# One-core hybrid block: order of the difference tables around the coefficient store, place of one output weight slice, order of two ScalarE copies at the start

## The reference, cut to what matters

```
h      = rmsnorm(x) * (1 + scale) + shift          # scale, shift, gate from silu(c) @ w_ada
u_pool, z_pool, u_ssm, z_ssm, g_pool, g_ssm = split(h @ w_in)
y_pool = pool_mixer(u_pool) * silu(z_pool)
y_ssm  = s5_mixer(u_ssm) * silu(z_ssm)             # complex diagonal state space, gelu, GLU
merged = sigmoid(g_pool) * (y_pool @ w_branch_pool) + sigmoid(g_ssm) * (y_ssm @ w_branch_ssm)
out    = x + gate * rmsnorm(merged @ w_out)
```

## Time and profile before

| | us |
|---|---|
| median of 3 runs | 964.11 |
| lowest and highest | 963.69, 964.80 |
| the profiled execution: its time | 963.69 |
| the profiled execution: its span | 961.9 |
| TensorE busy in the span | 940.3 |
| VectorE, ScalarE busy | 652.8, 349.9 |

### The profile page before, as it was taken

The page is one execution under the profiler, slowest core; times in us unless marked ns, Lnnn a source line. Parts: engine busy times, 40 slices in busy tenths (PEclk is TensorE's granted clock), DMA queues, the critical chain, the costliest instruction groups (busy, mean ns, idle before and its releaser), DMA issues.

```text
span 961.9 us, 11612 instructions
## 1 busy us (share of the span) xinstructions
PE 940.3 (98%) x4448; PEld 789.5 (82%) x4448; DVE 652.8 (68%) x914; ACT 349.9 (36%) x406; POOL 45.6 (5%) x82
## 2 busy tenths in 40 slices
PE   3999999999999999999999999999999999999997
PEld 3888878888888888888888888888888888788886
DVE  5988889988888868876797767654344444455233
ACT  6741442233333334545454554622022221133111
POOL 0019700000000000000000000000000000000000
PEclk9999999999999999999999999999999999999999
DMA  9753263445555379657566445895643264322222
GB/s 351 293 164 134 114 209 132 154 154 185 196 192 186 100 224 280 188 167 232 158 199 202 144 145 162 265 343 193 183 167 110 88 228 188 131 88 88 88 88 88
DMA packets 95687, 168.27 MB, mean 175 GB/s; under 512 B 37648, under 2 KB 54160, under 8 KB 95632
## 3 DMA queue, kind: packets, MB, share of 16 engines
q1 hardware_dynamic: 86272, 163.07, 50.8%
q10 hardware_dynamic: 9360, 4.46, 2.2%
HBM read 118.21 MB, written 49.28 MB: 174 GB/s over the span
## 4 chain that ended last, share of the span: by engine, by line
PE 97%; DVE 1%; DMA 1%; ACT 0%; issue 0%; SPq 0%; DVEq 0%
PE ps L1872 55%; PE ps L1979 17%; PE ps L2080 9%; PE psb L1979 5%; PE ps L2026 2%; PE psb L2015 1%; PE psb L2013 1%; PE psa L2001 1%; PE psa L1948 1%; PE psa L1872 1%; PE psb L1898 1%; DMA x_tok<-in_x 1%; PE psb L1948 0%; PE ps L1898 0%; PE psa L1898 0%; PE psa L2073 0%
## 5 line engine op out<-in xcount | busy, mean ns | idle before, releaser
L1872 PE MATMUL ps<-bop,w_hi 128*128 128x512 f32 x1312 | 352.3, 390 | 0.2 <-DVE bop L1372 0.2
L1872 PEld LDWEIGHTS ps<-bop,w_hi 128*128 128x128 f32 x1312 | 245.5, 188 | 51.0 <-issue 0.8
L1872 PE MATMUL ps<-bop,w_lo 128*128 128x512 f32 x656 | 202.0, 389 | 0.0
L1872 PEld LDWEIGHTS ps<-bop,w_lo 128*128 128x128 f32 x656 | 123.2, 188 | 25.7
L1324 DVE TENSOR_TENSOR w_lo<-raw,w_hi 128x1024 fp32r<-128x1024 f32 x49 | 60.4, 1232 | 59.9 <-ACT w_hi L989 59.7
L989 ACT ACTIVATE w_hi<-raw 128x1024 fp32r<-128x1024 f32 x49 | 51.7, 1057 | 92.4 <-PE ps L1872 82.6
L1979 PE MATMUL ps<-bop,r_hi 128*128 128x512 f32 x208 | 64.1, 389 | 0.0
L1979 PE MATMUL ps<-t_hi,r_hi 128*128 128x512 f32 x140 | 55.3, 395 | 0.3 <-issue 0.3
L1979 PE MATMUL ps<-t_hi,r_lo 128*128 128x512 f32 x140 | 54.6, 390 | 0.0
L1979 PE MATMUL ps<-t_lo,r_hi 128*128 128x512 f32 x140 | 54.5, 389 | 0.0
L2080 PE MATMUL ps<-wo_hi,y_hi 128*128 128x512 f32 x128 | 49.8, 389 | 0.0
(11 more groups left out here) (317 smaller groups left out, 1544.5 us busy)
## 6 DMA issues: line engine op xcount, KB each, us to landing
raw<-in_wstream SPq DMA_DIRECT2D x58, 512.0 KB, 5.4
pair_raw<-in_wstream SPq DMA_DIRECT2D x20, 512.0 KB, 4.6
ada<-in_w_ada SPq DMA_DIRECT2D x16, 512.0 KB, 11.4
x_tok<-in_x SPq DMA_DIRECT2D x8, 512.0 KB, 6.2
gs_d<-gt SPq DMA_DIRECT2D x8, 512.0 KB, 4.5
win_d<-win_new SPq DMA_DIRECT2D x8, 512.0 KB, 4.0
wout_d<-wout_new SPq DMA_DIRECT2D x8, 512.0 KB, 5.6
wout<-wout_d SPq DMA_DIRECT2D x8, 512.0 KB, 3.9
```

What stands on the lines that cost most here:

```text
L1872: last = mm(ps[slot(u)][:, f * HALF:f * HALF + HALF], a[:, k, :], b(k, f), start=k == 0 and q == 0, stop=k == KT - 1 and q == 2)
```

## The change

Four things change. `xt_out(6)` and `split_hi(2)` swap places on ScalarE. On ScalarE `t_high(2)` moves behind the first two `pair_high`. On VectorE `t_low(1)` and `t_sums(3)` move from ahead of the first two `pair_low` to behind them, `t_low(2)` moves ahead of `sum1`, and `t_low(3)` ahead of `sum4`. The hi part of slice 3 of `w_out` moves from the first weight buffer into `bop`, so that `wo_high(3)` and `wo_low(3)` come after the last `bs` product; the wait for `raw_free[0]` goes, and `squares` takes the first weight buffer.

```diff
--- before.py
+++ after.py
@@ -184,7 +184,7 @@
         w_hi = [new(f"w_hi{s}", [P, KT, P], F32R) for s in range(2)]
         w_lo_at = cur[0]
         w_lo = [new(f"w_lo{s}", [P, KT, P], F32R) for s in range(2)]
-        squares = at("squares", [P, SEQ], raw_at + 3 * TILE)
+        squares = at("squares", [P, SEQ], raw_at)
         gt_at = cur[0]
         gt = [new(f"gt{s}", [P, SEQ]) for s in range(2)]
         mod_out = at("mod_out", [P, 2, D], gt_at)
@@ -235,8 +235,8 @@
         wo_lo = at("wo_lo", [P, KT, D], b_at, F32R)
         wo_hi_big = at("wo_hi", [P, KT, D], bop_at, F32R)
 
-        wo_hi_first = [at(f"wo_hi{n}", [P, D], raw_at + o * TILE, F32R) for n, o in enumerate((2, 4, 1, 0))]
-        wo_hi = [t[:, :] for t in wo_hi_first] + [wo_hi_big[:, n, :] for n in range(4, KT)]
+        wo_hi_first = [at(f"wo_hi{n}", [P, D], raw_at + o * TILE, F32R) for n, o in enumerate((2, 4, 1))]
+        wo_hi = [t[:, :] for t in wo_hi_first] + [wo_hi_big[:, n, :] for n in range(3, KT)]
 
 
         p1 = [0]
@@ -1042,10 +1042,10 @@
             for k in range(2, KT):
                 h_of(k)
                 h_high(k)
+                if k == 2:
+                    split_hi(2)
                 if k in (2, 3):
                     xt_out(k + 4)
-                if k == 2:
-                    split_hi(2)
             act.wait_ge(h_done, KT)
             fn(eye_c[:, :, 0:P], ident.unsqueeze(1).broadcast_to((P, GB, P)), ACT.Copy).then_inc(eye_ready, 1)
 
@@ -1126,9 +1126,9 @@
                 fn(ks[:, 0:6, :].rearrange("p (a g) h -> p a g h", a=2), six[:, :, :, P:P + SG], ACT.Copy)
                 fn(ks[:, 6:GB, :], two_[:, :, P:P + SG], ACT.Copy).then_inc(k_taken, 1)
 
-            t_high(2)
             pair_high(0, P1)
             pair_high(0, P2)
+            t_high(2)
             t_high(3)
             act.wait_ge(gs_stored[0], 16 * 4)
             evac(("zs", 0), gt[0][:, :], ACT.Silu)
@@ -1286,10 +1286,10 @@
                     act.wait_ge(row_done, 1)
                     fn(gate_row[:, :], psa[:, :], ACT.Copy).then_inc(row_ready, 1)
             act.wait_ge(raw_free[1], len(USES) // 2)
-            act.wait_ge(raw_free[0], (len(USES) + 1) // 2)
-            for n in range(4):
+            for n in range(3):
                 wo_high(n)
             act.wait_ge(mm_done, JOB["bs", 7] + 1)
+            wo_high(3)
             wo_high(4)
             m_high(KT - 1)
             for n in range(5, KT):
@@ -1427,9 +1427,6 @@
             t_sums(1)
             t_low(0)
             t_sums(2)
-            t_low(1)
-            dve.wait_ge(tabled, 1)
-            t_sums(3)
 
             def bcast(ap, axis, n):
                 shape = list(ap.shape)
@@ -1588,12 +1585,15 @@
 
             pair_low(0, P1)
             pair_low(0, P2)
+            t_low(1)
+            dve.wait_ge(tabled, 1)
+            t_sums(3)
+            t_low(2)
             dve.wait_ge(coef_stored, 16)
             sum1(0)
             sum2(0)
+            t_low(3)
             sum4(0)
-            t_low(2)
-            t_low(3)
             for i in (P6, P5, P3, P4):
                 pair_low(0, i)
             sum3(0)
@@ -1805,7 +1805,7 @@
             def merge(n):
                 q, last = n % 2, n == KT - 1
                 if last:
-                    for t in range(4):
+                    for t in range(3):
                         wo_low(t)
                 dve.wait_ge(g_in[q], 16 * (n // 2) + 16)
                 dve.wait_ge(mm_done, JOB["bs", n] + 1)
@@ -1814,7 +1814,8 @@
                 dve.wait_ge(reload_in[q], 16 * (n // 2) + 16)
                 tt(rt[q][:, :], gt[q][:, :], rt[q][:, :], ALU.add).then_inc(m_sum, 1)
                 if last:
-                    wo_low(4)
+                    for t in range(3, 5):
+                        wo_low(t)
                 dve.wait_ge(m_hi_done, n + 1)
                 tt(m_lo[:, n, :], rt[q][:, :], m_hi[:, n, :].bitcast(F32), ALU.subtract).then_inc(m_lo_done, 1)
```

## The result

The changed kernel takes 970.75 us in the median of 6 runs (968.16 to 971.60), the kernel before beside it 964.77 (963.69 to 965.23). The ratio of the means over all runs, of which the changed kernel has eight, is 1.0057, 95% interval 1.0043 to 1.0070: slower by 0.6%, 6.0 us by the medians and 5.5 by the means, where 967.5 us were forecast (range 966.1 to 969.4). Slower was right; the size was too small and the time lies outside the range. The profiled execution took 970.14 us with a span of 968.4, against 963.69 and 961.9.

A forecast was written before the change was run, and what follows sets the result against it. TensorE, busy 940.3 of 961.9 us, was taken as the bound. 963.69 + 2.9 (first pair) + 0 (start) + 0.75 (end) = 967.3, or 967.8 from the median 964.11; predicted 967.5, range 966.1 to 969.4.

The forecast's parts named there:

- VectorE's stall: First pair: VectorE stands still from 120.8 to about 125.35, 4.6 us, because pair_low(0, P1) needs pair_high(0, P1).
- each step behind it: First pair: durations added on VectorE and ScalarE; table load to 134.6, P2 at about 135.7, P6 at 138.5.
- both paths meet at P6: First pair: VectorE's and ScalarE's paths both let P6 start at 138.5, so they are not added.
- The size without the clock: First pair: P6 starts 2.9 us later, bounds 2.0 to 3.8, with no fall of the clock counted.
- The end: Output tile 0: wo_low(3) behind the merge makes the weight load of k=5 late; +0.75 us, bounds 0.5 to 0.95.
- the edit of the first pair could win at most 0.68: First pair, before: matmuls miss the pace by 0.10 + 0.30 + 0.28 = 0.68 us, all an edit there could win.
- the rival of the clock: TensorE may restart at half rate after the first pair's gap: 1.8 us more, 969.3 us; chance 0.13.
- The forecast gap: TensorE waits 2.8 to 3.3 us ahead of P2 of the first pair, with none to speak of ahead of P6.
- this half microsecond is not added: Start: block 7's transposes come 0.5 us late, but the wait ahead of P2 shrinks from 3.3 to 2.8 us; counted 0.

The follow-up runs named there:

- e4: The changed kernel with the evacuation of zs 0 ahead of t_high(3) on ScalarE: 969.26 us, ratio 1.0054.
- e3: The changed kernel with 14 unread matmuls between P1 and P2 of the first pair: 968.83 us, ratio 1.0052.
- e8: The kernel before with t_low(2) and t_low(3) moved ahead of sum4 on VectorE: 963.67 us, ratio 0.9994.
- e6: The kernel before with only the new order of t_high, t_low and t_sums: 969.42 us, ratio 1.0053.
- e2: The changed kernel with the start's order of xt_out(6) and split_hi(2) put back: 968.88 us, ratio 1.0052.
- e1: The changed kernel again, no edit: 970.39 us, ratio 1.0069 against the kernel before.
- e10: The changed kernel without the start's swap, 13 unread matmuls ahead of P2, and 9 more on TensorE ahead of the third product: 969.55 us.
- e9: The changed kernel without the start's swap and with 13 unread matmuls in the gap ahead of P2: 968.56 us.
- e5: The kernel before with only xt_out(6) and split_hi(2) swapped: 964.85 us, ratio 1.0007.
- e7: The kernel before with only slice 3 of w_out moved: 964.85 us, ratio 1.0009.

## Why the prediction was right and wrong

**Right.** VectorE's stall (4.6 us forecast, 4.51 measured), its cause, and each step behind it: with 1.05 us added for the later start, the forecast has pair_high(0, P1) at 125.78 and it was at 125.75, the table load at 134.35 (134.47), P2 at 136.75 (136.93). That both paths meet at P6, to within 0.3 us, is shown by e4. The size without the clock is e3's: P6 103.25 us behind the transposes of block 7, before 100.27; 2.98, with 0.1 of it the longer transposes of block 7, and 2.9 were forecast. The end was forecast at 0.75 and is 0.76 in the trace. That the edit of the first pair could win at most 0.68 was right too (0.58 won in e8).

**Wrong: the rival of the clock.** "The clock falls" had a chance of 0.13; it happened, and it is the largest part of the error. Its price was put at 1.8 us and is 1.6 in e3 and 2.4 in e6. The range ended at 969.4, 0.1 above the clock's case alone, so it had no room for this case and anything beside it. The argument against it was that the gap is a fifth of the first idle time. That says nothing of how little idleness is enough. The forecast gap of 2.8 to 3.3 us was short by a little as well; it was 3.44. In the five profiles with a gap of microseconds the clock stayed up behind 2.86 (e4) and 3.04 us (e2) and fell behind 3.15 (e1) and twice behind 3.44 (the changed kernel, e6). Length alone doesn't decide, though: behind one length, 3.44 us, the clock was low from 137.6 in one kernel and from 134.66 in the other, and two runs of the changed kernel, 968.16 and 968.45 us, have a mean clock of 0.999, as the kernel before has. By the Trainium skill, page "TensorE: Matmul & The Clock Gate", "Part 1: The HAM clock gate", the array is at half clock after idleness. The traces agree where the clock fell, 0.59 behind the gap and 1.00 where it is filled; behind the gaps of e2 and e4 the profiled executions show no fall.

**Wrong: "this half microsecond is not added".** The step took the coefficient store as a fixed point, "whose start is set by coef's store and not by TensorE". The store hangs on GpSimd, GpSimd on VectorE's angles, and VectorE has split_lo(3) among them, which waits for ScalarE's split_hi(3), and that for TensorE's second product. The chain after shows this path, and e10 that it passes the 2.04 us on, to within 0.3. Before, this wait was just met and left no idle time to read. The other traces agree. From the transposes of block 6 to VectorE's split of tile 3 it is 30.83 to 30.89 us in the six kernels with the swap, with 0.41 to 0.57 us of idle time ahead of it, and 30.35 to 30.52 in the seven without it, with none; in e10, where TensorE is held back, VectorE stands idle there for 2.08 us. From block 6 to the store's issue it is 85.08 to 85.44 us with the swap and 84.55 to 84.97 without, 0.35 apart in the mean. So most of the 0.5 stays in the time; that this holds for the time itself the medians don't show (e3 against e9, both filled, differ by 0.27 us, less than either scatters).

**The sum again.** 2.9 + 0.75 as forecast, + 1.6 for the clock + 0.5 for the start = 5.75. By the runs: 6.0 and 6.15 (e1); and of the parts alone e5 0.5, e6 5.1, e7 0.5, together 6.1. The profiled pair differs by 6.5 in the span since the x tiles of the second landed 0.54 us later. From the median of before as it stood in the same runs, 964.77, the corrected sum gives 970.5. That it comes so near is in part luck, since the clock's price differed between executions by more than that.

## What to carry to other kernels

When an in-order engine is to wait on something that lands late, put ahead of the wait all that doesn't need it; work moved behind such a wait can't begin until it ends, and here that cost more than the order among the moved pieces could ever win. If a forecast contains a gap of microseconds on TensorE, put the clock's fall in the sum and not among the unlikely cases, and ask what filling matmuls would bring. Before a delay is said to be absorbed at a later wait, follow that wait's own chain back past the point of the delay, through each split and copy that stands in the same queue.

## What the runs showed of the hardware

Fourteen matmuls without a use shorten the kernel by 1.6 us. Behind gaps of nearly one length the granted clock differed between kernels and between runs of one kernel: the mean over the span was between 0.994 and 0.999 in the runs of the changed kernel, for instance at 971.1 and 968.2 us; with the gap filled it was 0.999 to 1.000 (e3), and 0.998 to 1.000 in the kernel before beside it. Behind two gaps of the same 3.44 us the fall came 2.0 us behind the last matmul in one execution and 0.7 us behind the first matmul after the gap in the other, and cost 2.4 and 1.6 us. What decides when and whether it falls was not tried further and stays open. At the very start the transposes come at half pace under a printed clock of 1.00; behind the gap at 137 us the print shows the fall.
